# Twelve weight chunks kept in ring slots for both token tiles instead of six, with fewer slots for the gathered expert rows

## The reference, cut to what matters

```python
def peer_ffn(h, w_q, sub_keys, u, v):
    ...
    q = (xf @ w_q).reshape(T, P_HEADS, 2, P_QDIM // 2)
    s1 = jnp.einsum('thd,kd->thk', q[:, :, 0], sub_keys[0])
    s2 = jnp.einsum('thd,kd->thk', q[:, :, 1], sub_keys[1])
    ...
    eidx = (e1 * P_NKEYS + e2).reshape(T, P_HEADS * P_TOPK)
    ...
        hb = jnp.einsum('td,tkd->tk', xb, u[ib])
        act = jax.nn.gelu(hb, approximate=False) * gb
        return jnp.einsum('tk,tkd->td', act, v[ib])
```

## Time and profile before

| what | value |
|---|---|
| time, median of 3 runs | 1577.43 us (1577.22 to 1577.82) |
| profiled execution, its own time | 1578.89 us |
| its span, first to last instruction | 1577.2 us |
| VectorE busy | 1100.9 us (70%) |
| TensorE matmuls busy | 1064.4 us (67%) |
| GpSimd busy | 688.6 us (44%) |
| ScalarE busy | 515.4 us (33%) |
| moved by DMA | 615.95 MB, mean 391 GB/s |
| chain that ended last | DMA 70%, DVE 13%, PE 11% |

### The profile page before, as it was taken

One profiled execution on the slowest core, in us unless ns is written; L12 is line 12 of the kernel. 1 busy time (PEld: TensorE's weight loads), 2 busy tenths in 40 slices (PEclk: granted clock), 3 DMA queues, 4 the chain that ended last, 5 costly groups with the idle time before them and its releaser, 6 DMA issues.

```text
span 1577.2 us, 20727 instructions
## 1 busy us (share of the span) xinstructions
PE 1064.4 (67%) x6998; PEld 527.5 (33%) x6998; DVE 1100.9 (70%) x2839; ACT 515.4 (33%) x1569; POOL 688.6 (44%) x566
## 2 busy tenths in 40 slices
PE   6999856776656476766656778656766657555655
PEld 6796433333312133322333345312433313111111
DVE  1745566788878578996457889899548877744555
ACT  2221414333322334424323444424233233322223
POOL 0002434444444365685343436565334345445552
PEclk9999979887878688779788789967887879877677
DMA  9056999999999999999999999999999999999996
GB/s 382 22 174 234 368 421 421 420 421 421 421 415 421 421 394 412 419 391 422 421 421 421 421 421 408 418 405 421 420 421 417 419 416 412 417 409 421 421 421 274
DMA packets 86027, 615.95 MB, mean 391 GB/s; under 512 B 9504, under 2 KB 10272, under 8 KB 12704
## 3 DMA queue, kind: packets, MB, share of 16 engines
q0 software_dynamic: 73728, 536.90, 82.5%
q1 hardware_dynamic: 12048, 77.45, 12.2%
q10 hardware_dynamic: 144, 0.26, 0.0%
HBM read 613.53 MB, written 1.05 MB: 390 GB/s over the span
## 4 chain that ended last, share of the span: by engine, by line
DMA 70%; DVE 13%; PE 11%; ACT 2%; issue 1%; DVEq 1%; ACTq 0%; POOL 0%; POOLq 0%
DMA ring<-experts_dram,idx_now 70%; PE pm L1212 6%; DVE ring L1015 5%; DVE conv_buf L1084 4%; PE side L1466 2%; PE side L1212 1%; ACT L647 0%; ACT diag_all L636 0%; PE pm L1355 0%; DVE top_i L935 0%; DVE x_tok L1029 0%; DVE onehot L936 0%; ACT act_v L630 0%; DMA x_tok<-x_dram 0%; POOL ring L472 0%
## 5 line engine op out<-in xcount | busy, mean ns | idle before, releaser
L472 POOL DMA_INDIRECT ring<-experts_dram,idx_now x512 | 670.5, 1309 | 736.8 <-DMA ring<-experts_dram,idx_now 469.0
L1466 PE MATMUL side<-ring,diag_all 64*64 64x512 f32 x2056 | 663.3, 786 | 480.6 <-ACT diag_all L636 473.8
L1015 DVE SCALAR_TENSOR_TENSOR ring<-ring,h_tok 128x1024 f32<-128x1024 f32 x512 | 611.0, 1223 | 246.7 <-DMA ring<-experts_dram,idx_now 239.8
L1466 PE MATMUL pm<-ring,diag_all 64*64 64x512 f32 x2040 | 659.9, 788 | 0.0
L1466 PEld LDWEIGHTS side<-ring,diag_all 64*64 64x64 f32 x2056 | 156.4, 164 | 922.4 <-ACT diag_all L636 662.7
L627 ACT ACTIVATE ge<-hb 128x2 f32<-128x2 f32 (+1 forms) x257 | 52.2, 203 | 813.3 <-DVE ring L1015 812.8
L636 ACT ACTIVATE diag_all<-ident,act_v 128x64 f32<-128x64 f32 x512 | 150.5, 340 | 21.6 <-issue 0.7
L1466 PEld LDWEIGHTS pm<-ring,diag_all 64*64 64x64 f32 x2040 | 155.0, 165 | 0.0
L630 ACT ACTIVATE act_v<-ge,gates 128x1 f32<-128x1 f32 x512 | 123.7, 287 | 18.4 <-issue 0.7
L1084 DVE SCALAR_TENSOR_TENSOR conv_buf<-conv_buf,chan_sb 128x128 f32<-128x128 f32 x480 | 128.9, 344 | 0.0
L1212 PEld LDWEIGHTS side<-h_t,wbuf 128*128 128x128 f32 x640 | 73.5, 194 | 9.5 <-issue 9.5
(11 more groups left out here) (204 smaller groups left out, 930.8 us busy)
## 6 DMA issues: line engine op xcount, KB each, us to landing
wbuf<-wq_dram SPq DMA_DIRECT2D x24, 1024.0 KB, 10.3
wbuf<-w_dram SPq DMA_DIRECT2D x16, 1024.0 KB, 9.6
ring<-w_in_dram SPq DMA_DIRECT2D x5, 2048.0 KB, 22.1
wbuf<-w_o_dram SPq DMA_DIRECT2D x8, 1024.0 KB, 7.9
ring<-experts_dram,idx_now POOLq DMA_INDIRECT x512, 11.7
ring<-w_dram SPq DMA_DIRECT2D x4, 1024.0 KB, 14.9
gain<-gains_dram SPq DMA_DIRECT2D x7, 512.0 KB, 13.9
ring<-wq_dram SPq DMA_DIRECT2D x2, 1024.0 KB, 9.1
```

The costliest lines, as they stand in the source:

```text
L472: pool.indirect_dma_start(ring[:, r, :], None, table[layer], bass.IndirectOffsetOnAxis(idx_now[:, i % 2, n - n0:n - n0 + 1], 0)) \
L1015: dve.scalar_tensor_tensor(out=ring[:, slot, 0:D], in0=ring[:, slot, 0:D], scalar=1.0, in1=h_tok[:, t, :], op0=ALU.mult, op1=ALU.mult, acc ...
L1466: step = pe.matmul(acc[odd][c][j * HALF:(j + 1) * HALF, :], diag[rows, r % (2 * BATCH), :], ring[rows, slot, D + c * COLS:D + (c + 1) * COLS],
```

## The change

Twelve chunks are kept in place of six. Chunks 2 and 3 of the layer 0 queries are loaded once, into slots 14 and 15, and serve phases 0 and 1. Six `w1` chunks (not four) are kept, in slots 14, 15, 12, 13, 10, 11. Four query chunks of layer 1 (4, 5 in slots 8 and 9; 6, 7 in slots 14 and 15) are kept, not two. The table `AWAY` says from and to which pick a slot is closed to picks: slots 14 and 15 from pick 14 to 415, slots 10 to 13 from pick 128 to 295, slots 8 and 9 from pick 224 to 391. `load_kept` waits for the last use of the chunk that is in the slot, or for the last pick in it; slots 14 and 15 at first wait for `b_t_ready` 2, the end of the mixer's use of that part of the ring. The order of SP's loads is changed accordingly, and GpSimd's first pick in a returned slot waits for the last use of the chunk there.

```diff
-KEPT = 4
-KEPT_IN = {("w1", c): RING - KEPT + c for c in range(KEPT)} | {("q", 6): RING - KEPT, ("q", 7): RING - KEPT + 1}
-KEPT_FROM = PICKS
-KEPT_TO = {RING - KEPT + c: 3 * PICKS + 2 * RING if c < 2 else 2 * PICKS + 2 * RING + 8 for c in range(KEPT)}
+KEPT = [("q", 0, 2, 14), ("q", 0, 3, 15), ("w1", 0, 0, 14), ("w1", 0, 1, 15), ("w1", 0, 2, 12), ("w1", 0, 3, 13),
+        ("w1", 0, 4, 10), ("w1", 0, 5, 11), ("q", 2, 4, 8), ("q", 2, 5, 9), ("q", 2, 6, 14), ("q", 2, 7, 15)]
+KEPT_IN = {(kind, p, c): r for kind, p, c, r in KEPT}
+AWAY = {8: (PICKS + 6 * RING, 3 * PICKS + 8), 9: (PICKS + 6 * RING, 3 * PICKS + 8), 10: (PICKS, 2 * PICKS + 2 * RING + 8), 11: (PICKS, 2 * PICKS + 2 * RING + 8), 12: (PICKS, 2 * PICKS + 2 * RING + 8), 13: (PICKS, 2 * PICKS + 2 * RING + 8), 14: (RING - 2, 3 * PICKS + 2 * RING), 15: (RING - 2, 3 * PICKS + 2 * RING)}
...
-        free = [r for r in range(RING) if r not in KEPT_TO or not KEPT_FROM <= n < KEPT_TO[r]]
+        free = [r for r in range(RING) if r not in AWAY or not AWAY[r][0] <= n < AWAY[r][1]]
...
+                r, n = KEPT_IN[(kind, p, c)], KEPT.index((kind, p, c, KEPT_IN[(kind, p, c)]))
+                held = [k for k in KEPT[:n] if k[3] == r]
+                if held:
+                    sp.wait_ge(*last_use(*held[-1][:3]))
+                elif AWAY[r][0] < RING:
+                    sp.wait_ge(b_t_ready, 2)
                 else:
-                    sp.wait_ge(pw_ps, KD + r - RING + KEPT + 1)
+                    sp.wait_ge(v_multiplied, RING + max(n for n in range(AWAY[r][0]) if SLOTS[n][0] == r) + 1)
...
-            load_chunks("q", 0, 0, 4)
-            load_chunks("o", 1, 0, 4)
+            load_chunks("q", 0, 0, 2)
+            load_chunks("o", 1, 0, 2)
+            for c in (2, 3):
+                load_kept("q", 0, c)
+            load_chunks("o", 1, 2, 4)
             load_chunks("q", 0, 4, 8)
             load_gain("norm", 4)
-            load_chunks("q", 1, 0, 4)
+            load_chunks("q", 1, 0, 2)
             load_gain("bias", 0)
-            for c in range(KEPT):
+            for c in range(6):
                 load_kept("w1", 0, c)
-            load_chunks("w1", 0, KEPT, KD)
+            load_chunks("w1", 0, 6, KD)
             load_gain("norm", 5)
             load_chunks("w2", 0, 0, 4)
             load_chunks("q", 2, 0, 2)
             load_gain("norm", 6)
-            load_chunks("q", 2, 2, 6)
+            load_chunks("q", 2, 2, 4)
+            for c in (4, 5):
+                load_kept("q", 2, c)
             load_gain("bias", 1)
             for c in (6, 7):
                 load_kept("q", 2, c)
-            load_chunks("w1", 1, KEPT, KD)
+            load_chunks("w1", 1, 6, KD)
...
-            load_chunks("q", 3, 2, 6)
+            load_chunks("q", 3, 2, 4)
```

More of the change, by code:

```diff
@@ L57, with kept_as, kept_use @@
 X_OF_NORM = [0, 0, 1, 2, 3, 4, 5, 6, 7, 8]
-KEPT = 4
-KEPT_IN = {("w1", c): RING - KEPT + c for c in range(KEPT)} | {("q", 6): RING - KEPT, ("q", 7): RING - KEPT + 1}
-KEPT_FROM = PICKS
-KEPT_TO = {RING - KEPT + c: 3 * PICKS + 2 * RING if c < 2 else 2 * PICKS + 2 * RING + 8 for c in range(KEPT)}
+KEPT = [("q", 0, 2, 14), ("q", 0, 3, 15), ("w1", 0, 0, 14), ("w1", 0, 1, 15), ("w1", 0, 2, 12), ("w1", 0, 3, 13),
+        ("w1", 0, 4, 10), ("w1", 0, 5, 11), ("q", 2, 4, 8), ("q", 2, 5, 9), ("q", 2, 6, 14), ("q", 2, 7, 15)]
+KEPT_IN = {(kind, p, c): r for kind, p, c, r in KEPT}
+AWAY = {8: (PICKS + 6 * RING, 3 * PICKS + 8), 9: (PICKS + 6 * RING, 3 * PICKS + 8), 10: (PICKS, 2 * PICKS + 2 * RING + 8), 11: (PICKS, 2 * PICKS + 2 * RING + 8), 12: (PICKS, 2 * PICKS + 2 * RING + 8), 13: (PICKS, 2 * PICKS + 2 * RING + 8), 14: (RING - 2, 3 * PICKS + 2 * RING), 15: (RING - 2, 3 * PICKS + 2 * RING)}
+def kept_as(kind, p, c):
+    of = {"w1": 0, "q": p // 2 * 2}.get(kind)
+    return (kind, of, c) if (kind, of, c) in KEPT_IN else None
+def kept_use(key):
+    r = KEPT_IN[key]
+    return 16 * ([k[:3] for k in KEPT if k[3] == r].index(key) + 1)
 def weight_chunks():
-    order = [("o", 0, c) for c in range(4)] + [("q", 0, h) for h in range(4)]
-    order += [("o", 1, c) for c in range(4)] + [("q", 0, h) for h in range(4, 8)] + [("q", 1, h) for h in range(4)]
+    order = [("o", 0, c) for c in range(4)] + [("q", 0, 0), ("q", 0, 1)]
+    order += [("o", 1, c) for c in range(4)] + [("q", 0, h) for h in range(4, 8)] + [("q", 1, 0), ("q", 1, 1)]
     for p in (1, 2):
-        order += [("w1", p - 1, c) for c in range(KEPT, KD)] + [("w2", p - 1, c) for c in range(4)]
+        order += [("w1", p - 1, c) for c in range(KD)] + [("w2", p - 1, c) for c in range(4)]
         order += [("q", p + 1, h) for h in range(6)]
-    return order
+    return [chunk for chunk in order if not kept_as(*chunk)]
 CHUNKS = weight_chunks()
@@ L280, in hybrid_decoder_trunk_kernel @@
         gathered = [sem(f"gathered{r}") for r in range(RING)]
-        kept_loaded = [sem(f"kept_loaded{c}") for c in range(KEPT)]
+        kept_loaded = {r: sem(f"kept_loaded{r}") for r in AWAY}
         idx_copied, may_gather = sem("idx_copied"), sem("may_gather")
@@ L360, in multiplied, with last_use @@
                 return (wo_ps if kind == "o" else w2_ps), p * 4 + c + 1
+            def last_use(kind, p, c):
+                if kind == "w1":
+                    return pw_ps, KD + c + 1
+                return q_ps, nth_head(p + 1, c // 2, c % 2)
             def load_kept(kind, p, c):
-                r = KEPT_IN[(kind, c)]
-                if kind == "w1":
-                    sp.wait_ge(v_multiplied, RING + max(n for n in range(KEPT_FROM) if SLOTS[n][0] == r) + 1)
+                r, n = KEPT_IN[(kind, p, c)], KEPT.index((kind, p, c, KEPT_IN[(kind, p, c)]))
[4 more added lines that the diff above has]
+                    sp.wait_ge(b_t_ready, 2)
                 else:
-                    sp.wait_ge(pw_ps, KD + r - RING + KEPT + 1)
+                    sp.wait_ge(v_multiplied, RING + max(n for n in range(AWAY[r][0]) if SLOTS[n][0] == r) + 1)
                 view = {"q": wq_l[p // 2], "w1": w1}[kind]
-                sp.dma_start(ring[:, r, :], view[:, c, :]).then_inc(kept_loaded[r - RING + KEPT], 16)
+                sp.dma_start(ring[:, r, :], view[:, c, :]).then_inc(kept_loaded[r], 16)
             def load_chunks(kind, p, first, end):
@@ L465, in gathers @@
                                 pool.wait_ge(b_t_ready, 2)
-                        if r >= RING - KEPT and n >= KEPT_TO[r] and all(SLOTS[m][0] != r for m in range(KEPT_TO[r], n)):
-                            c = r - RING + KEPT
-                            pool.wait_ge(*((q_ps, nth_head(3, 3, c)) if c < 2 else (pw_ps, KD + c + 1)))
+                        if r in AWAY and n >= AWAY[r][1] and all(SLOTS[m][0] != r for m in range(AWAY[r][1], n)):
+                            kind, of, c = [k[:3] for k in KEPT if k[3] == r][-1]
+                            pool.wait_ge(*((pw_ps, KD + c + 1) if kind == "w1" else (q_ps, nth_head(of + 1, c // 2, c % 2))))
                         if n >= AHEAD:
@@ L1367, in chunk @@
             def chunk(kind, p, c):
[L1369 to L1372, removed]
+                key = kept_as(kind, p, c)
+                if key:
+                    pe.wait_ge(kept_loaded[KEPT_IN[key]], kept_use(key))
+                    return ring[:, KEPT_IN[key], :].rearrange("p (k c) -> p k c", k=KD)
                 n = CHUNKS.index((kind, p, c))
```

## The result

| | before | after |
|---|---|---|
| median | 1578.7 us (6 runs, 1577.22 to 1579.87) | 1589.19 us (6 runs, 1585.06 to 1593.65) |
| ratio after/before | | 1.0063, 95% interval 1.0048 to 1.0078 |
| profiled execution, its span | 1577.2 us | 1583.3 us |
| moved by DMA | 615.95 MB | 609.65 MB |

The change makes the kernel 0.63% slower, about 9.9 us (0.0063 x 1579; interval 7.6 to 12.3). It lies inside the stated range of 1565 to 1592, above the forecast of 1578, and on the side that had a chance of 0.36. It lies outside the forecast's own range of 1572 to 1585. One execution of e10 (1663.84 us, at a granted clock of 0.674 where its others have 0.82 to 0.83) is not counted in its ratio.

The account below looks back on a forecast made before the run. It took DMA bytes after about 190 us plus DMA idle time as the bound. Terms -14.9 for dropped loads and +15.0 for eight slots gave +0.1, plus 1.2 for the start, so +1: 1578 us, range 1565 to 1592 (own range 1572 to 1585).

Parts of the forecast that it names:

- The bound: Whole span: time is the bytes to move after about 190 us plus every stretch with DMA engines idle.
- rival B: Picks 224 to 295: each of four two-head query pairs stalls everything, 4 x 7.5 = 30 us, 1592.5; chance 0.25.
- forecast case: Whole kernel: idle DMA time about equals the saving, +1 us to 1578, range 1572 to 1585; chance 0.38.
- The removed loads: Phases 1 and 3 and tile 1: six dropped loads at 2.49 us each save 14.9 us if the lead is kept.
- The eight slots: Picks 224 to 295, 775 to 978 us: 8 slots for 12 cost +15.0 us of idle DMA time.
- two stocks of three picks above eight: At 852 and 932 us: 11 slots held, three above eight can't be fetched ahead, 7.5 us idle each time.
- A: Picks 224 to 295: eight slots cost only +5 us, slices stay at 415 or more, 1567.5; rival's chance 0.33.
- Ten slots at 0: Picks 136 to 223, about 514 to 772 us: 10 slots for 12 cost 0, bounds 0 to +3.
- The start at 0 to 2.5: Phase 0: q 2 and 3 wait for b_t_ready, land 0 to 2.5 us late; taken as 0, bounds -2 to +2.5.
- Picks 300 to 391, 12 slots for 14: 0 ... From there equal.: Picks 300 to 391: two fewer slots cost 0, bounds 0 to +3, and nothing differs afterwards.
- chunks 0 and 1 would go from 510 to near 391 us at no cost: SP's w1 loads: chunks 0 and 1 move just behind q 1 of phase 1, where the dropped pair was; 0.
- C: Start: kept loads of phase 0 delay first queries and all behind, 2.5 to 5 us extra, 1582; rival's chance 0.04.

Follow-up runs that it names:

- e10: Changed kernel, with w1 chunks 6 and 7 of tile 0 loaded only once w1 4 and 5 are multiplied, their old place; 1.0033 to before, +5.2 us.
- e2: Kernel before with its wide ring, the six dropped loads bringing only 1/16 of their bytes (output not the reference's); 0.9908 to before, -14.5 us.
- e1: Kernel before with all its loads, but as few slots for picks as the changed kernel at every pick; 1.0093 to before, +14.7 us.
- e8: Kernel before with all its loads and ten slots for picks, not 12, from pick 128 to 295; 1.0010 to before, +1.6 us.
- e9: Changed kernel, two-head query blocks of rounds 6 and 7 in phases 1 and 2 split into one head at a time; 1.0048 to before.
- e6: Changed kernel with only q 2 and 3 of layer 0 newly kept, two loads dropped, four w1 chunks as before; 0.9968 to before, -5.1 us.
- e4: Changed kernel with slots returned later: 10 to 13 from pick 304 (was 296), 8 and 9 from 402 (was 392); 1.0019 to before, +3.0 us.
- e12: Changed kernel with later slot return, split queries and w1 6 and 7 at their old place, six loads dropped; 0.9981 to before, -3.0 us.

## Why the prediction was right or wrong

**The bound, right.** The time is the bytes after the start plus the standing time of the DMA engines. The account of the four dips gives +6.8 us where the two executions differ by 6.1.

**The number, in range by luck.** 1589.19 (or 1577.4 x 1.0063 = 1587.3 on the base of the forecast) lies inside 1565 to 1592 only because rival B reached that far, and B is not what happened. The forecast case ended at 1585. It had +1 us against before, and the change costs 9.9.

**The removed loads, right.** -14.9 was forecast, e2 has -14.5 for 15/16 of it. The figure of about 358 GB/s, from the Trainium skill's page "DMA: Bandwidth & Descriptors", section Specifications, would have made 17.6 (16.5 for 15/16). The interval of e2 does not exclude that, but the slices at 421 GB/s do. The table has the figure as half of what two cores share, and here one core runs, so the trace does not go against the page as I had written.

**The eight slots, right in price and place, the mechanism not borne out.** "+15.0" was the term; e1 gives +14.7 for the whole ring, e8 leaves some 13 of it to the step from ten to eight, and after has (417 - 387)/421 x 140 = 10.0 us of it between 845 and 985. I had derived it from two stocks of three picks above eight, and given the query block of 7.41 us as the cause of the first. The ring was full through that block; but e9 has 3.84 and 4.76 us in its place, the waits stay at 56 us, and the rate does not rise. The counting of held slots was good, its story was not, and what fills the ring stays open.

**The rivals, wrong by their own signs.** A wanted the slices of 845 to 930 us at 415 or more; they have 389, 362 and 385. B wanted VectorE to wait 5 us or more after each pair of queries. VectorE's longest wait for a gather from 775 to 985 us is 3.7 us, and e9, with two of B's four blocks split, is not clearly faster.

**Ten slots at 0, right.** e8: +1.6, interval over zero. **The start at 0 to 2.5, right**: e6 keeps the whole saving of its pair, and the first queries out of the ring start at 177.4 us in after, 1.0 later than the 176.4 of before.

**What failed: "Picks 300 to 391, 12 slots for 14: 0 ... From there equal."** I counted slots there and not the wait with which a slot comes back. The front part of the document names that wait, and I did not cost it. It is 7 us of what is missing: after less e4 is 0.44%. Place and size: 4.8 us at 1000.6 and 9.1 us at 1264.2. Slots 12 and 13, returned at pick 296, hang on `w1` 2 and 3, as slots 14 and 15 did before; the added slots 10 and 11 hang on `w1` 4 and 5, used up to pick 291, and are handed out first.

**A second omission: the `w1` loads.** I wrote that chunks 0 and 1 would go from 510 to near 391 us at no cost. They went to 471.55, since they wait for the last use of `q` 2 and 3, and this is late in phase 0. And I did not see that keeping six makes `w1` 6 and 7 follow at once, 100 us earlier than before, into a stretch where VectorE waits for gathers. I had looked at just such a move for `q` 4 and 5 of phase 2. The DMA rows price it at 4.8 us, e10's ratio at 4.7, with intervals that overlap, so that its place is shown and its size is not.

The terms together: -15.5 (e2, scaled to the full bytes) + 14.7 (e1) + 7 (e4) + 4.7 (e10) = +10.9; measured +9.9. Each measured term is uncertain by 3 to 4 us, so the agreement to 1 us is partly chance; e12 bears the sum out from the other side. The chance of 0.36 for slower was held mainly by rival B, which is not what happened. The shares that I gave don't add up to it either: B, C and a quarter of the forecast case are 0.25 + 0.04 + 0.095 = 0.385, and what is left of the forecast case for "within" is 0.21 and not 0.27.

**What would show it.** The fall near 845 to 930 us to "near 390" came (389, 362, 385). VectorE's waits for gathers came too, at 849 to 859 us and at 954 to 968. GpSimd's waits for slots grew by 57 us and not 15: waiting at a full ring with gathers in flight is no standing time, and I had set them equal. "If the ring stalls show before 775 or after 1000, my counts misled me": they did show, and it was not the counts but two waits and a pair of moved loads.

## What to carry to other kernels

A buffer that is lent to something else has three prices: the narrower ring while it is away, the wait with which it comes back, and the loads behind it in the queue that now start earlier. The first was sized here from the held slots (issued less freed) of the old trace, though the reason given for it did not hold; the second needs the distance between the issue of a gather and its use: hand a slot back only as many picks after its last other use as the gathers run ahead. Dropped bytes pay in full where the transfers bound the end. Bytes moved out of a stretch where compute leads leave the DMA engines idle there: by the DMA rates the two moved loads cost here 4.8 us, about the 5.0 of two added ones, though the times do not resolve it.

## What was not expected

Closing the slots longer (e4) made the kernel 7 us faster: this program issues its gathers in the order of the picks, so that one gather that waits stops all behind it. And the price of the ring is far from linear: 1.6 us for the two slots from twelve to ten, some 13 for those from ten to eight, when at 852 us 11 had been held.
